# Second projection, Fourier mix and low-rank products in one part, with the units in another order

## What is computed

```python
def token_mixer(h, hc, w_in, ...):
    u = h @ w_in                                  # 512 positions
    uc = hc @ w_in[:, FOURIER_W:]                 # 256 context positions
    prep_l = rwkv_inputs(u[..., FOURIER_W:], ...)
    prep_c = rwkv_inputs(uc, ...)
    ...                                           # the recurrence over both, then
    out = concatenate([fourier_mix(u[..., :FOURIER_W], f_g), rw_l]) @ w_out

def fourier_mix(u, g):                            # 8 groups of 64 channels
    y = fft2(uf, axes=(1, 3), norm="ortho").real
    return rms_norm_2(y.reshape(b, t, 512), g)

def rwkv_inputs(u, conv_w, w0, w2, a0, a2, k_k, k_a):
    rkv = conv1d_centred(u[..., :1536], conv_w)   # three taps
    r, k, v = split(rkv, 3)
    w_lora = w0 + tanh(wd) @ w2                   # decay, per direction, rank 64
    decay = exp(-exp(-softplus(-w_lora) - 0.5))
    a = sigmoid(a0 + ad @ a2)                     # rate, per direction, rank 64
    kk = k * k_k                                  # per head of 64
    kk = kk * rsqrt(sum(kk * kk) + 1e-12)
    kd = k * (1 + (a - 1) * k_a)
    return r, kd, v, kk, a, decay, gd
```

## Time and profile before

| | us |
|---|---|
| median of 3 runs | 2192.63 (2187.82 to 2192.97) |
| profiled execution, its own time | 2192.46 |
| its span in the trace | 2190.3 |
| PE busy | 2016.2 (92%) |
| DVE busy | 808.0 (37%) |
| ACT busy | 458.2 (21%) |
| POOL busy | 193.8 (9%) |

### The profile page before, as it was taken

The page is one execution under the profiler, slowest core; times in us unless marked ns, Lnnn a source line. Parts: engine busy times, 40 slices in busy tenths (PEclk is TensorE's granted clock), DMA queues, the critical chain, the costliest instruction groups (busy, mean ns, idle before and its releaser), DMA issues.

```text
span 2190.3 us, 33103 instructions
## 1 busy us (share of the span) xinstructions
PE 2016.2 (92%) x13434; PEld 1055.8 (48%) x13434; DVE 808.0 (37%) x1525; ACT 458.2 (21%) x964; POOL 193.8 (9%) x274
## 2 busy tenths in 40 slices
PE   6995898899999999999899995988888899999996
PEld 2443775243444444444245543888853344444442
DVE  1702243302000000002322335776652588888102
ACT  1110265201000000001321133444430222221000
POOL 0000010010000000000100002654511000000000
PEclk9997598999999999999999996999998999999998
DMA  5321001523222222223431200000011122222222
GB/s 227 115 67 48 1 1 49 176 89 98 77 76 76 77 86 77 87 87 100 168 147 48 67 10 16 5 4 4 5 45 58 59 76 76 77 77 77 77 86 86
DMA packets 41831, 157.73 MB, mean 72 GB/s; under 512 B 4792, under 2 KB 5448, under 8 KB 40568
## 3 DMA queue, kind: packets, MB, share of 16 engines
q1 hardware_dynamic: 35856, 132.14, 18.5%
q10 hardware_dynamic: 5864, 23.94, 2.9%
HBM read 151.32 MB, written 6.31 MB: 72 GB/s over the span
## 4 chain that ended last, share of the span: by engine, by line
PE 72%; DVE 6%; ACT 2%; issue 1%; POOL 1%; DMA 0%; ACTq 0%; DVEq 0%; POOLq 0%
PE psum L331 37%; PE psum L1093 19%; PE psum L896 4%; PE psum L1730 2%; PE psum L1734 1%; PE psum L1515 1%; DVE mem L1889 1%; DVE mem L1917 1%; PE psum L1189 1%; PE psum L1741 1%; DVE mem L2201 1%; DVE mem L1916 1%; PE psum L1762 1%; ACT mem L2025 1%; PE psum L1558 0%
## 5 line engine op out<-in xcount | busy, mean ns | idle before, releaser
L331 PE MATMUL psum<-mem 128*128 128x512 f32 (+1 forms) x2272 | 950.1, 580 | 15.3 <-ACT mem L379 10.0
L331 PEld LDWEIGHTS psum<-mem 128*128 128x128 f32 x2272 | 431.2, 190 | 532.5 <-issue 520.6
L1093 PE MATMUL psum<-mem 128*128 128x512 f32 x960 | 420.1, 598 | 12.7 <-DVE mem L2209 10.9
L1093 PEld LDWEIGHTS psum<-mem 128*128 128x128 f32 x960 | 183.2, 191 | 248.5 <-issue 231.5
L2290 DVE SCALAR_TENSOR_TENSOR mem<-mem 128x512 f32<-128x512 f32 x352 | 235.1, 747 | 0.0
L384 POOL TENSOR_TENSOR mem<-mem 128x512 f32<-128x512 f32 x30 | 38.1, 1268 | 1200.6 <-ACT mem L369 1200.2
L1164 DVE TENSOR_TENSOR mem<-mem,psum 128x512 f32 x22 | 15.2, 690 | 285.9 <-PE psum L331 285.9
L369 ACT ACTIVATE mem<-mem 128x512 f32<-128x512 f32 x56 | 33.7, 626 | 415.2 <-DVE mem L1108 207.4
L1106 DVE TENSOR_TENSOR mem<-mem,psum 128x512 f32 x16 | 11.0, 688 | 214.4 <-PE psum L1093 214.4
L896 PE MATMUL psum<-mem 128*2 128x512 f32 x192 | 88.8, 613 | 0.0
L1730 PE MATMUL psum<-mem 64*64 64x64 f32 x1920 | 74.9, 222 | 12.5 <-DVE mem L1917 5.0
(11 more groups left out here) (287 smaller groups left out, 1790.5 us busy)
## 6 DMA issues: line engine op xcount, KB each, us to landing
mem<-in_units SPq DMA_DIRECT2D x248, 512.0 KB, 3.5
mem<-in_cw ACTq DMA_DIRECT2D x2, 2048.0 KB, 23.3
mem<-in_wn ACTq DMA_DIRECT2D x1, 2144.0 KB, 17.7
mem<-in_xT ACTq DMA_DIRECT2D x1, 2048.0 KB
bias_tiles<-bias_scratch ACTq DMA_DIRECT2D x1, 2048.0 KB
mem<-bias_tiles ACTq DMA_DIRECT2D x1, 2048.0 KB, 9.9
x_scratch<-mem ACTq DMA_DIRECT2D x1, 2048.0 KB, 8.5
mem<-in_dft ACTq DMA_DIRECT2D x1, 2048.0 KB, 14.0
```

Of the source, the lines that this page charges most:

```text
L331: last = pe.matmul(dst, ring[:, slot, k, :], rhs(k), start=(k == 0), stop=(k == 7))
L1093: last = eng.matmul(ps[m % 4], ring[:, slot, k - 8 * part, :], rhs(k), start=(k == 0), stop=(k == ktiles - 1))
```

## The change

`project2`, `fourier` and `low_rank` become one part. Its 19 units stand in another order (`PLACES`): the two low-rank inputs, the four Fourier inputs, k, v, the gate, r; the weights are laid out to match. Units 0, 1 and 6 to 13 have the context half. Behind each unit PE does what the tables give for its place: first and second Fourier products, decay products, key sums, rate products; ACT and DVE have their steps in the same loop.

Units use two PSUM banks and context halves two, where there were four each; decays and key sums use banks 4 and 5, Fourier 6 and 7, rates both pairs by turns. `raw` has three slots, so a copy into it waits until the taps three units back are done. The tanh is put in place in `lowT`, the sigmoid of a rate directly in `kka`, and DVE turns it into `kd` and `kka` with every step waited for. The Fourier output goes to `fT` unscaled and is scaled there. Several buffers lie elsewhere: `mixed` and the squares in `xT`, which therefore must have been stored first (`x_out`), `dft` and `ksq` in `kka`, `kroot` and `krec` in `kd`.

```diff
@@ -1270,29 +1270,29 @@
-        raw = r5.take(12, RAW)
-        dft = r5.take(2, 4, S)
...
+        r_kka = Region(kka[0].offset, kd0.offset)
+        dft = r_kka.take(2, 4, S)
+        ksq = r_kka.take(2, T2)
+        r_kd = Region(kd0.offset, kd0.offset + 12 * 4 * C)
+        kroot = r_kd.take(2, T2)
+        krec = r_kd.take(2, T2)
+        r_x = Region(xT.offset, xT.offset + KT * S)
+        mixed = r_x.take(4, 2, S)
+        r_x = Region(xT.offset, xT.offset + KT * S)
+        fsq = r_x.take(4, S)
+        scaled_a = r_x.take(T2)
+        r_sqr = Region(sqr.offset, sqr.offset + KT * S)
+        raw = r_sqr.take(3, RAW)
+        dft64 = r_sqr.take(256)
+        wl = r_sqr.take(512)
+        al = r_sqr.take(512)
+        lowT = Region(yC.offset, yC.offset + 2 * T2).take(2, T2)
...
@@ -1305,7 +1305,7 @@
-                eng.sem_inc(sem("in2_free"), 4)
+                eng.sem_inc(sem("in2_free"), 2)
...
@@ -1331,90 +1331,219 @@
+            NP = 19
+            rkv = (4, 5, 6, 7, 8, 9, 10, 11, 0, 1, 2, 3)
+            PLACES = [("low", 0), ("low", 1)] + [("f", n) for n in range(4)] + [("rkv", n) for n in range(8)] + [
+                ("gate", 0)] + [("rkv", n) for n in range(8, 12)]
+            with_ctx = [p for p, (kind, n) in enumerate(PLACES) if kind == "low" or kind == "rkv" and n < 8]
+            place_of = {kn: p for p, kn in enumerate(PLACES)}
+
+            def after(p, table):
+
+                return table.get(p, ())
+
+            DECAYS = {p: (p - 2,) for p in range(2, 10)}
+            FIRSTS = {p: (p - 3,) for p in range(3, 7)}
+            SECONDS = {p: (p - 8,) for p in range(8, 12)}
+            KEYS = {p: (p - 10,) for p in range(10, 14)}
+            USES = {16: (0, 1), 17: (2, 3), 18: (4, 5)}
+            RATES = {13: (0,), 14: (1, 2), 15: (3, 4), 16: (5, 6), 17: (7,)}
...
+                def unit(p):
                     def f(slot, j, i):
-                        eng.wait_ge(free, m + 1)
-                        last = product(eng, slot, lambda k: hT[:, k, CTX:T2], ps[m % 4], ready)
-                        if m in both:
-                            eng.wait_ge(free_ctx, m - 3)
-                            last = product(eng, slot, lambda k: hT[:, k, 0:CTX], ps[4 + m % 4][:, 0:CTX],
+                        eng.wait_ge(free, p + 1)
+                        last = product(eng, slot, lambda k: hT[:, k, CTX:T2], ps[p % 2], ready)
+                        if p in with_ctx:
+                            c = with_ctx.index(p)
+                            eng.wait_ge(free_ctx, c + 1)
+                            last = product(eng, slot, lambda k: hT[:, k, 0:CTX], ps[2 + c % 2][:, 0:CTX],
                                            lambda eng, k: eng.wait_ge(ctx_shifted, k + 1))
                         return last
-                    return f
-
-                def key_sums(hp):
+                    per_unit(eng, u0 + p, 1, f)
...
+                def rate(n):
+                    d, hp = n // 4, n % 4
+                    r = slice(64 * d, 64 * d + 64)
+                    if n == 0:
+                        eng.wait_ge(f_varied, 1)
+                    elif n == 1:
+                        eng.wait_ge(varied, 4)
+                    else:
+                        eng.wait_ge(rate_kept, n - 1)
+                    low_rank(rate_bank(n), al[r, hp * P:(hp + 1) * P], lowT[r, 1], rated)
...
+                def key_sum(hp):
                     eng.wait_ge(squared, hp + 1)
-                    if hp >= 2:
-                        eng.wait_ge(varied, hp - 1)
-                    b = 4 + 2 * (hp % 2)
-                    eng.matmul(ps[b], ones64, ksq[:, hp % 2, 0:512], start=True, stop=True)
-                    eng.matmul(ps[b + 1][:, 0:256], ones64, ksq[:, hp % 2, 512:T2], start=True, stop=True).then_inc(summed, 1)
-
-                for m in range(19):
-                    per_unit(eng, u0 + m, 1, use(m))
-                    if m in (15, 17):
-                        eng.wait_ge(free_ctx, 14)
-                        for hp in (m - 15, m - 14):
-                            key_sums(hp)
+                    if hp == 0:
+                        eng.wait_ge(decay_kept, 8)
+                    else:
+                        eng.wait_ge(varied, hp)
+                    a, b = pair(4)
...
+                for p in range(NP):
+                    unit(p)
+                    for ct in after(p, FIRSTS):
+                        dft_first(ct)
+                    for ct in after(p, SECONDS):
+                        dft_second(ct)
+                    for n in after(p, DECAYS):
+                        decay(n)
+                    if p == 12:
+                        dft_sum()
+                    for hp in after(p, KEYS):
+                        key_sum(hp)
+                    for n in after(p, RATES):
+                        rate(n)
...
+                def keep_main(p):
+                    kind, n = PLACES[p]
+                    eng.wait_ge(units_done, u0 + p + 1)
+                    if kind == "rkv" and n >= 3:
+                        eng.wait_ge(conv_done, n - 2)
+                    eng.copy(main_dst(p), ps[p % 2]).then_inc(free, 1)
...
+                def keep_rate(n):
+                    d, hp = n // 4, n % 4
+                    a, b = pair(rate_bank(n))
+                    eng.wait_ge(rated, n + 1)
+                    if n == 0:
+                        eng.wait_ge(summed, 4)
...
@@ -1422,175 +1551,106 @@
+                    if p == 1:
+                        eng.wait_ge(free, 4)
+                        eng.wait_ge(free_ctx, 4)
+                        eng.activation(lowT[:, 0], lowT[:, 0], ACT.Tanh).then_inc(low_ready, 1)
+                    if p == 3:
+                        arrived(eng, "x_out")
+                    kind, n = PLACES[p - 1]
+                    if p and kind == "rkv":
+                        first_taps(n)
+                    for ct in after(p, FIRSTS):
+                        keep_first(ct)
+                    for ct in after(p, SECONDS):
+                        keep_second(ct)
+                    for n in after(p, DECAYS):
+                        keep_decay(n)
+                    if 9 <= p <= 12:
+                        key_squares(p - 9)
+                    if p == 11:
+                        eng.wait_ge(second_kept, 4)
+                        for ct in range(4):
+                            eng.activation(fsq[:, ct, :], fT[:, ct, :], ACT.Square).then_inc(f_squared, 1)
+                    if p == 13:
+                        eng.wait_ge(f_varied, 1)
+                        eng.activation(rstd2, rstd, ACT.Sqrt).then_inc(f_rooted, 1)
+                    if 11 <= p <= 14:
+                        key_roots(p - 11)
+                    for n in after(p, RATES):
+                        keep_rate(n)
+                first_taps(11)
             def dve(eng, steps):
+                def taps(n):
+                    for i, (dst, src_, c) in enumerate(pieces(n)):
+                        eng.wait_ge(tapped, n_pieces(n) + i + 1)
+                        for tap in (1, 2):
+                            steps.link(eng.scalar_tensor_tensor(dst, view(src_, tap, [[C, c], [1, C]]),
+                                                                col("rconv", 12 * tap + rkv[n]), dst, ALU.mult, ALU.add))
+                    eng.sem_inc(conv_done, 1)
...
+                def key_var(hp):
+                    a, b = pair(4)
+                    eng.wait_ge(summed, hp + 1)
+                    if hp >= 2:
+                        eng.wait_ge(made_kk, hp - 1)
+                    eng.tensor_scalar(kroot[:, hp % 2, 0:512], a, 1e-12, None, ALU.add)
...
+                def rates(n):
+                    d, hp = n // 4, n % 4
+                    a = kka[d][:, :, hp, :]
+                    eng.wait_ge(rate_kept, n + 1)
+                    eng.wait_ge(made_kk, 4)
+                    steps.link(eng.tensor_scalar(chunks(scaled_a), a, col("k_a", hp), omka[:, hp:hp + 1], ALU.mult, ALU.add))
+                    steps.link(eng.tensor_tensor(kd[d][:, :, hp, :], kC[:, :, hp, :], chunks(scaled_a), ALU.mult))
+                    steps.link(eng.tensor_tensor(a, kkC[:, :, hp, :], a, ALU.mult))
...
+                for p in range(NP):
+                    kind, n = PLACES[p]
+                    if p in with_ctx:
+                        eng.wait_ge(units_done, u0 + p + 1)
+                        eng.tensor_copy(ctx_dst(p), ps[2 + with_ctx.index(p) % 2][:, 0:CTX]).then_inc(free_ctx, 1)
+                    kind, n = PLACES[p - 1]
+                    if p and kind == "rkv":
+                        taps(n)
+                        if n < 4:
+                            key_scale(n)
+                    if 11 <= p <= 14:
+                        key_var(p - 11)
+                    if p == 13:
+                        eng.wait_ge(f_summed, 1)
+                        eng.tensor_scalar(rstd, ps[6], 1.0 / 512, EPS, ALU.mult, ALU.add).then_inc(f_varied, 1)
```

(59 more changed lines are left out.)

262 lines of the change are left out of this document (71 added, 191 removed).

## The result

The changed kernel took 2210.73 us (median of ten runs, 2201.78 to 2215.51), the kernel before 2189.44 on the same chip (ten runs, 2184.99 to 2197.78). The ratio is 1.0083, 95% interval 1.0063 to 1.0102: slower by more than the 0.3% named in the prediction. The profiled execution took 2210.57; its span is 17.9 us longer than that of before. The predicted 2201.5 had the right sign and half of the size, and the measured median is above the upper end of the range, 2208.

A forecast was written before the change was run, and what follows sets the result against it. PE was taken to bound most of the 254.7 us stretch, with hand-overs to DVE late. New costs 1.7 + 5.2 + 5.2 + 15.1 + 5.0 = 32.2 against 23.2 removed gave +9.0: 2192.5 to 2201.5 us, range 2191 to 2208.

The forecast's parts named there:

- the waits: PE idle at key sums 2 and 3 and before rate 1 (places 12, 13, 14): 1.7, 5.2 and 5.2 us.
- T + 5.2: Places 12 to 14: DVE's key variance releases PE 5.2 us after T, the end of PE's unit there.
- place 2: First decay product: PE might wait there for the low-rank weights' load; taken as 0, with 2 us as other end.
- Rival (c): Whole stretch: PE is never made to wait, leaving PE's work plus tail; -8.1 us, 2184.4; chance 0.08.
- Rival (d): Places 13 and 14: waits half as long and the clock falls once; 24.5 against 23.2, 2193.8 us; chance 0.10.
- 2.5 us each: Behind the gaps at places 13 and 14: about 5 us of work at half clock each, 5.0 us lost in all.
- rival (b): Clock stays low for long (+5.2), or place 2 or 12 adds its own cost; 2204 to 2210 us; chance 0.16.
- the gap of 1.7: Place 12, PE's wait at key sum 2: lies between the clock rows, so no fall of the clock was taken.
- The tail: Behind PE's last unit: DVE's last taps and four uses of rates, with PE idle, 15.1 us.
- PE's work, 231.5: From project2's first product: units, key sums, Fourier and low-rank products at full clock, summed from old durations, 231.5 us.
- the 23.2 that the change could win: Old stretch of 254.7 us less PE's work of 231.5: idle time and half clock, all taken as removed.
- Activation tables: Places 11 to 14: Sqrt and Sigmoid alternate, six loads instead of three, 1.28 us each, cost 0.

The follow-up runs named there:

- experiment 1: Changed kernel with DVE's key variances and Fourier variance ahead of the context copy and taps of their place: 2193.78 us, ratio 0.9995 to the kernel before.
- experiment 6: experiment 5 with decays, key norms and rate products one place earlier and Fourier's scalings behind the stage barrier: 2178.23 us, ratio 0.9921 to the kernel before.
- experiment 7: Kernel before, with four unread 512-column matmuls in PE's 3.9 us wait for the Fourier output: 2187.09 us, ratio 0.9964 to the kernel before.
- experiment 5: experiment 1 with rate uses begun a place sooner and the last four units' taps in their own place: 2190.5 us, ratio 0.9979 to the kernel before.
- experiment 2: Changed kernel with only the key variances ahead of the taps, Fourier's variance still behind them: one run, 2196.56 us.

## Why the prediction was right or wrong

**What bounds it, and the waits: right.** Places, releasers and lengths came as worked out: 1.76, 5.27 and 5.18 us against 1.7, 5.2 and 5.2. T + 5.2, built from four steps of the old trace, was the release at T + 5.27. No gap stood ahead of place 12. At place 2 the low-rank weights, issued at 1110.34 and 13.3 us in landing, were there at about 1123.6, and the decay product follows the unit directly at 1124.30 (forecast 0, other end 2). Rival (c), PE never waits, is what experiment 1 (but for 1.38 us) and experiment 6 (entirely) then made true by another order. Rival (d), a variance that doesn't wait for both pieces of the taps, didn't occur.

**The clock: right that it falls at both gaps and not at the third, wrong in the lengths.** The step that failed is "2.5 us each": 1.5 and 5.1 us were lost. It took the length of a spell from the gap ahead of it; these two came from gaps of nearly the same length. The 15.5 us spell over 64-row products had been read and put into rival (b), and was set aside because "a whole unit follows them". What counted was what came directly behind the gap: a 128-row key sum at place 13, two 64-row rate products at place 14. That the sum of both, 6.6, is still near 5.0 is luck: one was too high by 1.0 and the other too low by 2.6. To take no fall for the gap of 1.7 was right, but its nearest row above wasn't looked at: behind 2.62 us, in the kernel before, the clock did fall (experiment 7). The Trainium skill ("TensorE: Matmul & The Clock Gate", section "HAM oscillation — how this bites in real kernels") says that each gap between bursts pays the return of the clock again. The trace agrees in that both gaps over 5 us paid, and the 1.76 didn't; the two sizes, 3.0 and 10.2 us of half clock, are this trace's own.

**The tail: 15.1 forecast, 16.2 measured.** A use took 2.70 us instead of 2.65, and three small waits of 0.2 to 0.6 us stand ahead of taps and uses, where every step now waits for the one before. The term is right in kind and 1.1 short.

**The term that was missing: PE's work, 231.5.** This step failed most. It was summed from durations at the old places, where low-rank products stand behind one another and units behind one another, and has no term for the changes between 64 and 128 rows. They cost 5.0 us, 3.2 of it at the eight decays. The earlier trace rows held the prices without the change of size, and no row of before showed that change in the middle of a run of units. Two smaller errors stand beside it. The 231.5 isn't all at full clock, as it is called: its 172.8 hold the spell at the start of the stretch, 2.4 us of loss in the kernel before and 1.9 in the one after the earlier trace rows. And its sixteen products at 1.29 are 1.3 us too much, in the old order as in the new, as two of them run at the same time; the 23.2 that the change could win is as much too small. With the gains of 0.6 and 1.3, the work comes out 3.5 above the forecast and not 5.

**Outside the stretch.** 17.9 us of span are 15.3 in the stretch, 2.0 ahead of it and 0.6 behind. The code ahead of it is the same. The start of the stretch lay between 1086.4 and 1095.8 us over the profiles of all these kernels, which share that code, so a single profile says nothing on 2 us there. Whether the change makes that part slower at all stays open.

**The sum.** +15.3 against the forecast +9.0: PE's work 3.5, the clock 1.6, the tail 1.1, the waits 0.1. All four have one sign. The upper end of 2208 took one long spell or a load wait, but no term for work that costs more at another place, and was too low by 3. As for the mechanism, the forecast stands: removed idle time of 23.2 against new waits, tail and half clock of 35.0.

**Activation tables: right in number and cost, not in place.** Six loads of 1.28 us ran in the stretch, but only four from unit 12 on (1259.49, 1292.96, 1303.16, 1307.53); the other two came with the tanh and the first decay (1118.07, 1124.94). None is on the chain.

## What to carry to other kernels

When small work is threaded between large units, list for every engine the step that another engine waits for, and ask what stands ahead of it in its in-order queue: here two variances moved ahead of the taps took 17 us out of the stretch, and with the other steps moved as in experiments 5 and 6 the interleaving went from 0.8% slower to 0.8% faster. Sum up an interleaving with prices of the new neighbourhood, not of the old one, and give each gap that lets the clock fall its own price by what runs directly behind it. A gap that can't be removed can be filled with products nobody reads, which gave back 6 to 8 us here.

## What the runs showed of the hardware

- A change between weights of 64 and of 128 rows cost about 0.2 us each way in float32: the product 1.05 instead of 0.86, the unit behind it 7.07 instead of 6.87.
- Two 64-row products directly behind one another, the first on rows 0 to 63 of the weights and the second on rows 64 to 127, ran at the same time: 1.07 + 0.43 us for both instead of twice 1.29. In the kernel of experiment 6, where no such two are neighbours, no pair did.
- Behind the gap of 5.2 us at place 14 the granted clock stood at 0.50 for 10.1 to 10.3 us of work when 64-row products followed directly, and for 3.9 to 5.3 when the same products had 128 rows. Behind the gap of 5.3 us at place 13, which a 128-row key sum follows, it was 2.9 to 3.4 us in five of the six profiles and 6.1 in one.
- PE's waits of about 1 us (before), 1.38 (experiment 1) and 1.76 (after) left the clock at 1.00; one of 2.62 (before, with one of 0.77 and 2.0 us of work ahead of it) and one of 3.48 (experiment 2) made it fall.
